# A fused three-block transformer kernel whose TensorE no longer multiplies constants between a layer norm and the projection behind it

## The chip, the cores and the metric

The kernel runs on one core of a Trainium2 chip. The metric is the time of one execution on the device in microseconds (us). A core has TensorE (PE: matmuls and, as PEld, the loads of the stationary operand), VectorE (DVE), ScalarE (ACT), GpSimd (POOL) and SyncE (SP), which here issues the loads of the weights.

## The reference, cut to what matters

Three different blocks are applied to the same 256 tokens of width 2048, each with its own weights (about 600 MB in fp32 altogether). Each block is a large input projection, three or two token mixers, an output projection, and a residual layer norm; blocks two and three have a feed-forward part with a second layer norm. The change sits where a layer norm is followed by a projection of its result:

```
# block 1, end                          out = merged @ w_o
x = _layer_norm(ALPHA * x + out, ln_g, ln_b)
# block 2                               u = x @ w_in_2, mixers, then:
x = layer_norm(alpha * x + mix @ w_out_2, ln1_g, ln1_b)
gu = x @ w_gate_up_2;  hid = silu(gu[..., :D_FF]) * gu[..., D_FF:]
x = layer_norm(alpha * x + hid @ w_down_2, ln2_g, ln2_b)
# block 3                               proj = x @ w_in_3, mixers, then:
x = layer_norm_3(ALPHA * x + mixed @ w_out_3, ln1_g, ln1_b)
h = square(relu(x @ w_up_3))
x = layer_norm_3(ALPHA * x + h @ w_down_3, ln2_g, ln2_b)
```

The norm subtracts the mean over the 2048 columns of a token, multiplies by the inverse root of the variance, and applies gain and bias. So there are four places where a projection waits for a norm: in front of `cvg0` (first projection of block 2), `gu` (gate and up of block 2), `qkm` (first projection of block 3) and `up3`. The last norm is followed by the output only.

## The kernel before, in words

Every weight passes through a ring of four slots. SyncE loads a chunk of 256 rows by 512 columns, ScalarE rounds it to `w_hi` (L1282), VectorE computes the remainder `w_lo` (L1809), and TensorE multiplies in three products: hi by hi, hi by lo, lo by hi (`products`, L594 to L596; the "wide" kind has L618 for the first two at once and L624 for the third). A tile of a projection has eight chunks of two k-steps each; a chunk is 24 matmuls of 256 columns in the kinds F, or 8 of 512 and 8 of 256 columns in the wide kind.

The activations lie token-major in `xtok`. For a projection they are needed column-major: TensorE transposes them in eight groups (`transpose_x`, L746, four transposes a group, eight matmul rows for two groups), ScalarE copies a group to `x_hi` (L1331, `x_both` in the profile) and VectorE makes `x_lo` from it (L1809, also `x_both`), which frees the group for TensorE (semaphore `xTp_used`).

At a norm the last chunk of the projection ahead is computed in token halves, so that VectorE adds and measures one half (`half_done`) while TensorE computes the other. VectorE then takes the statistics, centres and scales the columns of chunk 0 in two finer quarters (`scaled(0, 2)`), each of which raises `x_cols`, and TensorE transposes group 0 and group 1, one for each. Chunk 0 of the projection then needs group 0 only. Columns for later groups are scaled by VectorE (L1815) while chunk 0 runs, and transposed ahead of chunks 1, 3 and 5.

`project_opening` (L679) writes this order for TensorE. All engines run their streams in program order. With `normed=True` it first waits on `tile_free` of the PSUM tile that the projection will write, then calls `keep_clock` (L674), which multiplies `upper` (a triangle of ones, constant) by the identity into that PSUM tile with start=True; chunk 0 starts the same tile anew, so the product is never read. Eight such products come ahead of the transposes of groups 0 and 1, two behind them. Each fp32 product is two matmul rows of 256 columns in the trace.

The diff touches `keep_clock` and `project_opening` alone. Of the five calls, `aqk` at the program's start is not normed and has no such products; `cvg0`, `gu` (wide), `qkm` and `up3` (wide) have.

Of the kernel before, what the change touches and what calls it, by code (L numbers as in the profile page):

```python
# [16 lines left out]
S = 256  # L17
# [152 lines left out]
def tiles_of(eng, sec, unroll=False, opens=False, closes=False):  # L170

    n, a, b = sec.n, sec.u0, 1 - sec.u0
    pairs = n // 2 - closes
    alone = pairs if unroll else min(1, pairs) if opens else 0
    if pairs - alone == 1:
        alone = pairs
    for i in range(alone):
        yield 2 * i, a, i
        yield 2 * i + 1, b, i
    if alone < pairs:  # L180
        with eng.Fori(alone, pairs) as i:
            yield 2 * i, a, i
            yield 2 * i + 1, b, i
    if closes:
        yield 2 * pairs, a, pairs
        yield 2 * pairs + 1, b, pairs
    if n % 2:
        yield n - 1, a, pairs


def build(nc, I, out):
    plan, widths, landed = plan_weights()
    ctx = ExitStack()
    with ctx:
        free = [-(-nc.sbuf_base // 32) * 32]

        def sb(name, shape, dt=F32, at=None):

            if at is None:
                at = free[0]  # L200
                free[0] += -(-4 * int(np.prod(shape[1:])) // 32) * 32
            return nc.alloc_sbuf_tensor_at(name, shape, dt, offset=at)
# [34 lines left out]
        ident = ident_r[:].bitcast(F32)  # L237
        ones = sb("ones", [P, P])
        upper = sb("upper", [P, S])
# [11 lines left out]
        ps = ctx.enter_context(nc.psum_tensor("ps", [P, 8, 512], F32))  # L251
# [337 lines left out]
        def _(pe):  # L589
# [72 lines left out]
            def stationary(hi, lo, at=0):  # L662

                return lambda c, s: [v[:, at + c * CH:at + (c + 1) * CH, :] for v in (hi, lo)]
# [6 lines left out]
                    tile(kind, u, sec.chunk(u, 0), sec.more(it), sec.chunks, src, width, side=side, halves=halves,  # L671
                         normed_next=norm and t == sec.n - 1)

            def keep_clock(u, times):  # L674

                for i in range(times):
                    pe.matmul(ps[:, 2 * u, 0:S], ident, upper[:, 0:S], start=True, stop=True)

            def project_opening(name, normed=True, side=None, kind="F"):  # L679

                sec, base = plan[name], n.now(xTp_used)
                if normed:
                    pe.wait_ge(tile_free[sec.u0], sec.tiles[sec.u0])
                    keep_clock(sec.u0, 8)
                    transpose_x(range(2), normed)
                    keep_clock(sec.u0, 2)
                else:
                    transpose_x(range(4), normed)
                for t, u, it in tiles_of(pe, sec, side is not None, opens=True):
                    first = isinstance(t, int) and t == 0  # L690
                    pe.wait_ge(tile_free[u], sec.tiles[u] + it)
                    tile(kind, u, sec.chunk(u, 0), sec.more(it), sec.chunks, stationary(x_hi, x_lo), TW,
                         (normed, base) if first else None, None if first else side, at=4 * (u ^ sec.u0))
# [42 lines left out]
            def transpose_x(groups, normed):  # L736

                for g in groups:
                    if normed and (g % 2 == 0 or g == 1):
                        pe.wait_ge(x_cols, n.next(x_cols))  # L740
                    elif g % 2 == 0 and not normed:
                        pe.wait_ge(x_landed[g // 2], 16)
                    pe.wait_ge(xTp_used, max(0, n.now(xTp_used, 1) - 3))
                    for k in range(2):
                        for t in range(2):
                            last = pe.transpose(ps[:, 4 + g % 4, k * S + t * P:k * S + (t + 1) * P].bitcast(F32R),  # L746
                                                xtok_r[:, t, (2 * g + k) * P:(2 * g + k + 1) * P], ident_r[:])
                    last.then_inc(xTp_ready, 1)
# [424 lines left out]

            pe.wait_ge(ident_ready, 1)
            project_opening("aqk", False)
            pe.wait_ge(par_landed, 16 * len(params))
            pe.wait_ge(xTp_used, n.now(xTp_used))
# [5 lines left out]
            for k in range(KT):  # L1183
                for i, (w, x) in enumerate(((alr_hi, x_hi), (alr_hi, x_lo), (alr_lo, x_hi))):
                    last = pe.matmul(ps[0:G_RANK, 6, 0:S], w[:, k, :], x[:, k, :], start=(k == 0 and i == 0),
                                     stop=(k == KT - 1 and i == 2))
# [11 lines left out]
            sec = plan["merge"]  # L1198
# [26 lines left out]
            project("wo", "T", merged, norm=True)  # L1225

            project_opening("cvg0")
            side = second_mixers()
            project("cvg1", "F", side=side, halves=True)
            project("qkv", "F", side=side, halves=True)  # L1230
            project("z", "F", side=side, halves=True)
            project("wout2", "T", in_parts((1, 1, 2, 2, 3, 3, 4, 4)), side=side, halves=True, norm=True)
            project_opening("gu", kind="wide")
            pe.wait_ge(h_primed, AHEAD)
            project("down2", "T", hidden, norm=True)
# [1587 lines left out]
```

## Time and profile before

| | |
|---|---|
| median of 3 runs | 3470.61 us (3467.54 to 3471.84) |
| profiled execution, time | 3468.43 us |
| its span | 3466.6 us (1.8 us outside it) |
| PE busy, share of the span | 3411.7 us, 98% |
| DVE, ACT | 2224.0 us (64%), 1632.0 us (47%) |
| mean granted TensorE clock | 0.996 |
| DMA | 609.04 MB, mean 176 GB/s |

TensorE is busy nearly all the time, so what lengthens its stream lengthens the kernel, and a busier VectorE or ScalarE does so only where TensorE waits for them. The page's waits and timelines show where. A granted clock of 1.00 is the higher of TensorE's two levels (2.4 GHz), 0.50 the lower (1.2 GHz).

### The profile page before, as it was taken

What the parts mean: (1) busy time and instruction counts of PE and PEld (TensorE: products, weight loads), DVE (VectorE), ACT (ScalarE), POOL (GpSimd) and SP (SyncE); (2) the same over time, 40 slices, a digit from 0 to 9 for tenths busy, and PEclk for the clock granted to TensorE, in tenths of its full rate; (3) what the DMA queues carried; (4) which work ended last, traced back from release to release, by engine and by line L of the source; (5) the groups of instructions that cost most, each with busy time, mean ns of one, the idle gap of its engine ahead of it and who ended that gap; (6) DMA issues with size and microseconds to landing.
All of it is one profiled execution on the core that took longest, in us unless ns stands there. A gap on an engine that the chain in (4) does not pass through costs nothing.

```text
span 3466.6 us, 50657 instructions
## 1 busy us (share of the span) xinstructions
PE 3411.7 (98%) x20440; PEld 3037.7 (88%) x20440; DVE 2224.0 (64%) x2895; ACT 1632.0 (47%) x1924; POOL 6.3 (0%) x9
## 2 busy tenths in 40 slices
PE   8999999999999999999999999999999999999998
PEld 8998998888889999888888888899999888888886
DVE  5777655555568997565455566777766645457766
ACT  4445544444434443544444455543444444555554
POOL 0000000000000000000000000000000000000000
PEclk9999999999999999999999999999999999999999
DMA  6454566566655522555655566545446566666664
GB/s 193 146 168 151 157 192 202 193 197 205 215 165 164 158 86 74 187 160 187 193 188 187 187 210 193 182 148 164 152 145 210 156 194 192 188 201 199 194 192 149
DMA packets 324193, 609.04 MB, mean 176 GB/s; under 512 B 28254, under 2 KB 42592, under 8 KB 322729
## 3 DMA queue, kind: packets, MB, share of 16 engines
q1 hardware_dynamic: 317640, 587.45, 54.0%
q10 hardware_dynamic: 6368, 19.01, 1.5%
q8 instruction: 131, 2.15, 0.2%
q14 instruction: 54, 0.43, 0.0%
HBM read 604.29 MB, written 2.10 MB: 175 GB/s over the span
## 4 chain that ended last, share of the span: by engine, by line
PE 90%; DVE 7%; ACT 1%; issue 1%; DMA 1%; SPq 0%; ACTq 0%; DVEq 0%
PE ps L594 20%; PE ps L595 20%; PE ps L596 20%; PE ps L618 16%; PE ps L624 8%; DVE xtok L1815 2%; DVE arena L1815 2%; DVE w_lo L1809 1%; DVE arena L1809 1%; PE ps L1099 1%; DMA ring<-in_w_in 1%; PE ps L1118 0%; ACT w_hi L1282 0%; PE ps L800 0%; PE ps L1115 0%
## 5 line engine op out<-in xcount | busy, mean ns | idle before, releaser
L1809 DVE TENSOR_TENSOR w_lo<-ring,w_hi 128x1024 fp32r<-128x1024 f32 (+2 forms) x1136 | 1367.2, 1209 | 1017.0 <-ACT w_hi L1282 836.5
L1282 ACT ACTIVATE w_hi<-ring 128x1024 fp32r<-128x1024 f32 (+2 forms) x1136 | 1183.3, 1047 | 1551.6 <-PE ps L594 1155.5
L594 PE MATMUL ps<-x_both,w_hi 128*128 128x256 f32 x2368 | 684.4, 289 | 1.7 <-DVE x_both L1809 1.4
L595 PE MATMUL ps<-x_both,w_hi 128*128 128x256 f32 x2368 | 672.3, 284 | 0.0
L596 PE MATMUL ps<-x_both,w_lo 128*128 128x256 f32 x2368 | 672.2, 284 | 0.0
L618 PE MATMUL ps<-x_both,w_hi 128*128 128x512 f32 x2432 | 610.0, 393 | 1.9 <-DVE x_both L1809 1.9
L618 PEld LDWEIGHTS ps<-x_both,w_hi 128*128 128x128 f32 x2432 | 437.4, 189 | 80.9 <-DVE x_both L1809 2.3
L594 PEld LDWEIGHTS ps<-x_both,w_hi 128*128 128x128 f32 x2368 | 456.2, 193 | 7.4 <-issue 4.8
L595 PEld LDWEIGHTS ps<-x_both,w_hi 128*128 128x128 f32 x2368 | 456.5, 193 | 0.8 <-issue 0.5
L596 PEld LDWEIGHTS ps<-x_both,w_lo 128*128 128x128 f32 x2368 | 456.0, 193 | 0.0
L624 PEld LDWEIGHTS ps<-x_both,w_lo 128*128 128x128 f32 x2432 | 331.8, 190 | 23.7
L624 PE MATMUL ps<-x_both,w_lo 128*128 128x256 f32 x2432 | 339.1, 282 | 0.0
L594 PE MATMUL ps<-w_hi,h_hi 128*128 128x512 f32 x864 | 336.5, 389 | 2.0 <-DVE h_lo L1809 2.0
L595 PE MATMUL ps<-w_lo,h_hi 128*128 128x512 f32 x864 | 336.3, 389 | 0.0
L596 PE MATMUL ps<-w_hi,h_lo 128*128 128x512 f32 x864 | 336.3, 389 | 0.0
L594 PE MATMUL ps<-w_hi,x_both 128*128 128x512 f32 (+1 forms) x672 | 259.2, 386 | 0.0
L596 PE MATMUL ps<-w_hi,x_both 128*128 128x512 f32 (+1 forms) x672 | 255.6, 380 | 0.0
L595 PE MATMUL ps<-w_lo,x_both 128*128 128x512 f32 (+1 forms) x672 | 255.4, 380 | 0.0
L594 PEld LDWEIGHTS ps<-w_hi,h_hi 128*128 128x128 f32 x864 | 162.2, 188 | 36.5 <-DVE h_lo L1809 2.8
L595 PEld LDWEIGHTS ps<-w_lo,h_hi 128*128 128x128 f32 x864 | 162.2, 188 | 33.5
L596 PEld LDWEIGHTS ps<-w_hi,h_lo 128*128 128x128 f32 x864 | 162.2, 188 | 33.5
L594 PE MATMUL ps<-w_hi,y_hi 128*128 128x512 f32 x448 | 174.7, 390 | 3.4 <-DVE y_lo L1809 3.4
(356 smaller groups left out, 3253.9 us busy)
## 6 DMA issues: line engine op xcount, KB each, us to landing
ring<-in_w_in SPq DMA_DIRECT2D x416, 512.0 KB, 3.5
ring<-in_w_down SPq DMA_DIRECT2D x216, 512.0 KB, 4.2
ring<-in_w_gate_up SPq DMA_DIRECT2D x176, 512.0 KB, 4.2
ring<-in_w_up SPq DMA_DIRECT2D x128, 512.0 KB, 3.9
ring<-in_w_out SPq DMA_DIRECT2D x64, 512.0 KB, 4.4
ring<-in_w_branch SPq DMA_DIRECT2D x36, 512.0 KB, 4.1
ring<-in_w_in SPq DMA_DIRECT2D x48, 384.0 KB, 3.0
ring<-in_w_o SPq DMA_DIRECT2D x32, 512.0 KB, 4.5
```

The lines of the kernel that those rows point to most:

```text
L594: first = pe.matmul(out, left[0], right[0], start=start, stop=False)
L595: pe.matmul(out, left[0], right[1], start=False, stop=False)
L596: return first, pe.matmul(out, left[1], right[0], start=False, stop=stop)
L618: first = pe.matmul(ps[:, at + e, :], w_hi[:, s, k, e * P:(e + 1) * P], x_both[:, c * CH + k].rearrange("p h s -> p (h s)"), start=(c == 0 ...
L624: last = pe.matmul(ps[:, at + e, 0:S], w_lo[:, s, k, e * P:(e + 1) * P], x_hi[:, c * CH + k, :], start=False, stop=(c == chunks - 1 and k ...
L1099: last = pe.matmul(ps[:, 4 + e, m * P:(m + 1) * P], d_lm[:, 4 * e + m], d_t[:, 8 * f + 4 * e + m], start=True, stop=True)
L1282: last = act.activation(w_hi[:, s, :, 0:width], ring[:, s, :, 0:width], ACT.Copy)
L1809: return dve.tensor_tensor(o, a, b, op)
L1815: return dve.scalar_tensor_tensor(o, a, s, b, op0, op1, **kw)
```

## The change

The helper `keep_clock` and its two calls are deleted. The waits, the transposes, the token halves at the norm, the finer quarter and the two groups ahead of chunk 0 stay as they are, and no other engine's code is touched.

```
             def project_opening(name, normed=True, side=None, kind="F"):
                 sec, base = plan[name], n.now(xTp_used)
                 if normed:
                     pe.wait_ge(tile_free[sec.u0], sec.tiles[sec.u0])
-                    keep_clock(sec.u0, 8)
                     transpose_x(range(2), normed)
-                    keep_clock(sec.u0, 2)
                 else:
                     transpose_x(range(4), normed)
...
-            def keep_clock(u, times):
-                for i in range(times):
-                    pe.matmul(ps[:, 2 * u, 0:S], ident, upper[:, 0:S], start=True, stop=True)
```

TensorE's order before, where the output projection of block 1 (`m_hi`, `m_lo` are its inputs) ends and `cvg0` begins:

```order
L595 MATMUL ps<-w_lo,m_hi 128x512
L596 MATMUL ps<-w_hi,m_lo 128x512
L677 MATMUL ps<-upper,ident_r 128x256 x8
L746 MATMUL ps<-ident_r,xtok_r 128x128 x8
L677 MATMUL ps<-upper,ident_r 128x256 x2
L594 MATMUL ps<-x_both,w_hi 128x256
```

And in the changed kernel, whose lines have moved up by seven:

```order
L595 MATMUL ps<-w_lo,m_hi 128x512
L596 MATMUL ps<-w_hi,m_lo 128x512
L739 MATMUL ps<-ident_r,xtok_r 128x128 x8
L594 MATMUL ps<-x_both,w_hi 128x256
```

Both rows of constants are gone; the transposes now follow the last product directly. It is the same at `qkm`. At `gu` and `up3` the row behind is the wide one; before:

```order
L677 MATMUL ps<-upper,ident_r 128x256 x8
L746 MATMUL ps<-ident_r,xtok_r 128x128 x8
L677 MATMUL ps<-upper,ident_r 128x256 x2
L618 MATMUL ps<-x_both,w_hi 128x512 x8
L624 MATMUL ps<-x_both,w_lo 128x256 x8
```

The rest of TensorE's stream is the same, 14112 rows before and 14104 now, and nothing moves on the other engines.

## Rows read from the trace of the kernel before

**Rows 1.** The page: busy time, granted clock by slice, chain that ended last.
```profile
PE 3411.7 (98%) x20440; PEld 3037.7 (88%) x20440; DVE 2224.0 (64%) x2895; ACT 1632.0 (47%) x1924; POOL 6.3 (0%) x9
...
PE 90%; DVE 7%; ACT 1%; issue 1%; DMA 1%; SPq 0%; ACTq 0%; DVEq 0%
```
**Rows 2.** Instructions of line 677: count, duration in ns (minimum/median/maximum), starts.
```profile
L677 PE MATMUL ps<-upper,ident_r x80: 377/379/634, 986.9 to 2738.4; 128*128 128x256 f32 x80
```
**Rows 3.** Timeline of PE at cvg0: start, length, operation, [idle before <-releaser], in us.
```profile
986.91 3.61 PE L677 MATMUL ps<-upper,ident_r 128*128 128x256 f32 x16
992.62 0.53 PE L746 MATMUL ps<-ident_r,xtok_r 128*128 128x128 f32 x4 [2.09 <-DVE xtok L1815]
993.41 0.53 PE L746 MATMUL ps<-ident_r,xtok_r 128*128 128x128 f32 x4 [0.26 <-DVE xtok L1815]
993.77 1.10 PE L677 MATMUL ps<-upper,ident_r 128*128 128x256 f32 x4
994.61 0.39 PE L594 MATMUL ps<-x_both,w_hi 128*128 128x256 f32 x1
...
998.12 0.88 PE L746 MATMUL ps<-ident_r,xtok_r 128*128 128x128 f32 x8 [0.39 <-DVE xtok L1815]
```
**Rows 4.** Chain of waits in time order at cvg0, and VectorE's timeline row of the same place.
```profile
994.60 0.69 DVE x_both L1809
...
993.81 1.48 DVE L1809 TENSOR_TENSOR x_both<-ps,x_both 128x512 fp32r<-128x512 f32 x2 [0.46 <-ACT x_both L1331]
```
**Rows 5.** Timeline of PE at qkm.
```profile
2239.42 3.61 PE L677 MATMUL ps<-upper,ident_r 128*128 128x256 f32 x16
2246.25 0.53 PE L746 MATMUL ps<-ident_r,xtok_r 128*128 128x128 f32 x4 [3.22 <-DVE xtok L1815]
...
2248.35 0.78 PE L594 MATMUL ps<-x_both,w_hi 128*128 128x256 f32 x1
...
2252.75 0.80 PE L746 MATMUL ps<-ident_r,xtok_r 128*128 128x128 f32 x8
```
**Rows 6.** Windows: busy time (xcount) of PE, PEld, DVE, ACT, POOL; granted clock; DMA share; GB/s.
```profile
990.35:994.61 4.26, 1.91 (x14) 1.44 (x13) 3.66 (x9) 1.43 (x3) 0.00 (x0) 1.00 0.00 0
...
2247.96:2251.37 3.41, 3.41 (x16) 3.24 (x15) 3.28 (x6) 1.30 (x2) 0.00 (x0) 0.50 0.00 0
...
1264.93:1268.33 3.40, 3.17 (x15) 3.18 (x16) 2.19 (x4) 0.60 (x1) 0.00 (x0) 0.50 0.08 12
...
1495.08:1502.79 7.71, 5.36 (x29) 4.29 (x28) 6.97 (x17) 1.49 (x3) 0.00 (x0) 1.00 0.25 88
2730.78:2738.48 7.70, 5.34 (x29) 4.28 (x28) 6.97 (x16) 1.49 (x3) 0.00 (x0) 1.00 0.30 98
```
**Rows 7.** Timeline of PE around 1265 us, in block 2.
```profile
1265.16 3.56 PE L1099 MATMUL ps<-arena 128*128 128x128 f32 x16 [3.04 <-DVE arena L1809]
```
**Rows 8.** Timeline of PE at the program's start.
```profile
6.33 1.23 PE L746 MATMUL ps<-ident_r,xtok_r 128*128 128x128 f32 x8 [6.33 <-DMA xtok<-in_x]
...
10.98 0.54 PE L594 MATMUL ps<-x_both,w_hi 128*128 128x256 f32 x1
...
15.37 0.41 PE L596 MATMUL ps<-x_both,w_lo 128*128 128x256 f32 x1
15.58 0.32 PE L594 MATMUL ps<-x_both,w_hi 128*128 128x256 f32 x1
...
18.26 0.28 PE L595 MATMUL ps<-x_both,w_hi 128*128 128x256 f32 x1
18.38 0.28 PE L596 MATMUL ps<-x_both,w_lo 128*128 128x256 f32 x1
```
**Rows 9.** Timeline of PE at gu.
```profile
1502.79 2.11 PE L618 MATMUL ps<-x_both,w_hi 128*128 128x512 f32 x8
...
1506.31 0.88 PE L746 MATMUL ps<-ident_r,xtok_r 128*128 128x128 f32 x8 [0.46 <-DVE xtok L1815]
...
1517.27 2.12 PE L618 MATMUL ps<-x_both,w_hi 128*128 128x512 f32 x8 [0.94 <-DVE x_both L1809]
```

More of the change, by code:

```diff
@@ L672, in project @@
                          normed_next=norm and t == sec.n - 1)
-            def keep_clock(u, times):
-                for i in range(times):
-                    pe.matmul(ps[:, 2 * u, 0:S], ident, upper[:, 0:S], start=True, stop=True)
             def project_opening(name, normed=True, side=None, kind="F"):
@@ L683, in project_opening @@
                     pe.wait_ge(tile_free[sec.u0], sec.tiles[sec.u0])
-                    keep_clock(sec.u0, 8)
                     transpose_x(range(2), normed)
-                    keep_clock(sec.u0, 2)
                 else:
```

## Prediction

> **What bounds the kernel now.** I read the page first. PE is busy for 98% of the span and makes up 90% of the chain that ended last [rows 1]: TensorE sets the time, so the question is what its stream loses or gains at the places that the diff touches. Next I read the instructions of line 677 [rows 2]: 80 matmul rows, that is 10 products of two rows at each of four openings (cvg0, gu, qkm, up3). Then the timeline of PE at one of them, cvg0 [rows 3]. The reader should see that it is not TensorE that is late there. The first 16 rows of constants start the moment the last product is issued and take 3.6 us; after them PE still sits idle for 2.09 us, then for 0.26 us, until VectorE delivers normalised columns. Only from chunk 0 on (994.61) does PE work in earnest, and 3.51 us later, at the transposes ahead of chunk 1, it waits once more for VectorE, 0.39 us. So the constants stand in time that is otherwise idle, and what they can do is act on TensorE's clock. That is why the windows view comes last, for its granted clock [rows 6].
>
> **The change, part by part.**
>
> *The eight products ahead of the transposes.* They are removed: 4 x 16 rows at 0.22 us each (3.61 us for 16), 3.5 us of PE time per opening. The cover is the norm on VectorE, which ends 2.09 us after them at cvg0 and 3.22 us after them at qkm [rows 3, 5]. Direct gain: nothing, at any of the four.
>
> *The two products behind the transposes.* They are removed too: four rows, 0.84 us from 993.77 to the start of chunk 0 at 994.61 [rows 3]. What they hide is the way of group 0 through ScalarE and VectorE. VectorE starts the first of its two x_both instructions at 993.81 and the second at 994.60 [rows 4], so the first result, which chunk 0 needs, is there between 994.5 and 994.6, and chunk 0 starts at 994.61. The products cost at most 0.1 us there. I take 0.05 us for each opening, 0.2 us in all; the bounds are 0 and 0.5 us. Nothing else waits behind them: no semaphore is raised by them.
>
> *What their absence does to the clock.* This is the term that matters, and no row shows an opening without constants. Before, cvg0, gu and up3 went through the gap up to chunk 0 at a granted clock of 1.00 [rows 6]. Without the constants PE has nothing from 986.9 to 994.5 at cvg0 but eight rows of transposes: 7.6 us. Two rows of this trace say what such a gap leads to. In block 2 PE waited 3.04 us for VectorE [rows 7], and the stretch of 3.4 us behind it ran at 0.50 [rows 6]. At qkm, whose norm comes 1.1 us later than the others, the idle time was 3.22 us in spite of the constants, and the clock was 0.50 from 2247.96 to 2251.37 [rows 5, 6]. Gaps with more than twice that idle time should fall to the lower level every time. I take it that all four do.
>
> *What a low opening costs.* The lower bound is qkm itself. From the start of chunk 0 to the next transposes it took 2252.75 - 2248.35 = 4.40 us [rows 5], cvg0 at full clock 998.12 - 994.61 = 3.51 us [rows 3]. The difference is 0.9 us: the matmuls were slower, but the 0.39 us wait for VectorE was swallowed. The upper bound comes from the program's start, where PE came out of idleness as it will now: the low clock lasted until 15.58, 4.6 us after the first product at 10.98, with matmuls 0.21 us apart instead of 0.12 [rows 8]. A chunk 0 wholly at that pace takes 24 x 0.21 = 5.1 us. The transposes ahead of it are slower as well: eight rows took 1.23 us there against 0.88 us [rows 8, 3], 0.35 for eight, so some 0.2 us for the four of a group, through which ScalarE and VectorE are reached later. Chunk 0 would begin at 994.8 and end at 999.9 in place of 998.12: 1.8 us, and 2.1 us if the transposes behind it are low as well. Where in the gap the clock falls decides between 0.9 and 2.1; the only full opening without constants (the start) speaks for the upper half and the only one at a norm for the lower, so I take 1.3 us. Wide openings are priced alike: chunk 0 is 3.52 us from start to transposes with a wait of 0.46 us in it [rows 9]. The later wait of 0.94 us at 1517.27 does not take the loss back, since VectorE, which ends it, is fed by the transposes that come late.
>
> *The sum.* cvg0, gu and up3 turn from full to low: 3 x 1.3 = 3.9 us (bounds 2.7 and 6.3). qkm was low already and has a longer gap now: 0.4 us more (bounds 0 and 1.2). The constants give back 0.2 us. Together +4.1 us on the profiled execution of 3468.43 us: 3472.5 us. The profiled execution lies 2.2 us below the median of 3470.61 us, but part of that distance may be openings of before that fell low in other executions, which would shrink the step there. I go half the way: 3473.5 us, +2.9 us or +0.08% on the median. The noise of the three runs is 4.3 us from end to end. A measurement of this kernel tells a change from none at about 0.2%, 6.9 us, so my forecast is within it.
>
> **The rivals.**
>
> *The clock does not fall, or does so as often as before.* For it: the level before was full through 2.09 us of idle time, and only one such gap in four fell. Against it: 3.04 and 3.22 us of idle time fell both times, and now there are over 5 us without a row of any kind. It would leave the 0.2 us gain: 3470.4 us, and 3468.2 us if the profiled execution is taken as the base. It is also the case in which the change does nothing at all to the path.
>
> *The clock comes back late* (the slower side). The place is chunk 1 and, in the F openings, chunk 2, where PE no longer waits for anyone, so that every low microsecond costs in full. If the clock stays low for one more stretch of 3.4 us at each opening, 3.4 x (1 - 0.12 / 0.21) = 1.5 us is lost on top of 2.1: 3.6 us an opening, 14.4 us in all, less the 0.9 that qkm pays already: +13.3 us, 3483.9 us. It decides (over 6.9 us in all) from a mean cost of 2.0 us an opening, which is when the clock comes back some 5 us or more after chunk 0 starts. For it: at the program's start it took 4.6 us, close to that point, and it had been low through the transposes too [rows 8]. Against it: at qkm and at 1265 us the low stretch was over after 3.4 us [rows 6], and the start had further pauses for the input ahead of its first chunk.
>
> On the same side stands a rule of the Trainium skill, page "TensorE: Matmul & The Clock Gate", section "Terms": the penalty is the throttled time multiplied by the share of clock pulses held back, which is a half at the lower level. By that rule 3.41 us at 0.50 would cost 1.7 us and two such stretches at each opening 3.4 us, 3.4 x 4 - 1.7 = +11.9 us in all, 3482.5 us. The row of qkm speaks against counting so: its 3.41 low microseconds cost 0.9 us, because 0.39 us of them came ahead of chunk 0 and TensorE had another 0.39 us of waiting to give away.
>
> *The constants cost more than they seem to.* If ScalarE and VectorE were ready well ahead of 994.6 and the second set was what chunk 0 waited for, removing it would give up to 0.84 us an opening, 3.4 us in all: 3467.2 us with the clock unhurt. Against it: the x_both rows end at that very moment [rows 4]. Even then it is not faster by 0.2%.
>
> **How the numbers follow.** All four openings low at 0.9 to 2.1 us: 0.62, forecast 3473.5 us, own range 3470 to 3478. Clock unhurt: 0.17, about 3470. Clock late: 0.16, from 3478 up; I cut its far end. Constants on the path: 0.02. Something not in the profile, either side: 0.03. The range of 3467.5 to 3480 us takes in the first, second and fourth case with the spread of the runs shown, and the near part of the third. Slower by over 0.2% (above 3477.5): the third case and a tail of the first, together 0.16, since part of the third stays below its price. Faster by over 0.2% (below 3463.7): 0.03. Within: 0.81.
>
> **What would show it.** In the changed profile: a granted clock of 0.50 in the stretch around the start of cvg0, gu, qkm and up3; idle time of 5.7 us (6.8 at qkm) ahead of the first transposes; first matmuls of chunk 0 spaced 0.21 us; from the start of chunk 0 to the next transposes 4.4 to 5.3 us in place of 3.5, without the 0.39 us wait; and chunk 0 starting 0.1 to 0.2 us later relative to the norm's last product, or 0.05 us earlier if the fall comes after it. The forecast is wrong if an opening keeps 1.00, if low stretches reach into chunk 2, or if the waits of VectorE for PE move so that the loss is made good behind the opening, by the next norm at the latest.

## The result and the profile after

| | before | after |
|---|---|---|
| median | 3470.52 us (3467.48 to 3473.63, 22 runs) | 3475.70 us (3472.55 to 3478.53, 22 runs) |
| ratio | | 1.0014, 95% interval 1.0008 to 1.0020 |
| profiled execution, span | 3468.43 us, 3466.6 us | 3475.74 us, 3473.9 us |
| mean granted clock | 0.996 | 0.991 |

The changed kernel is slower by 5.2 us at the median, 0.15%; the interval excludes zero and goes from 2.8 to 6.9 us. The forecast was 3473.5 us in a range of 3467.5 to 3480 us.

First the page of the kernel after: busy time of each engine. TensorE has less to do, and yet the kernel takes longer:

```profile
PE 3403.8 (98%) x20360; PEld 3030.2 (87%) x20360; DVE 2223.9 (64%) x2895; ACT 1632.3 (47%) x1924; POOL 6.3 (0%) x9
```

PE lost 80 rows against [rows 1], and 7.9 us of busy time. (The page counts 20440 rows before and 20360 now; the counts of 14112 and 14104 given with the change stand in no view of the trace.) VectorE and ScalarE have the same work. Now the four openings in the timeline of PE (start, length, operation, idle before it), each with its first transposes and those ahead of chunk 1:

```profile
992.82 1.50 PE L739 MATMUL ps<-ident_r,xtok_r 128*128 128x128 f32 x8 [5.59 <-issue]
995.01 0.55 PE L594 MATMUL ps<-x_both,w_hi 128*128 128x256 f32 x1 [0.69 <-issue]
...
1503.09 1.50 PE L739 MATMUL ps<-ident_r,xtok_r 128*128 128x128 f32 x8 [5.59 <-issue]
1505.27 3.75 PE L618 MATMUL ps<-x_both,w_hi 128*128 128x512 f32 x8 [0.68 <-issue]
...
1510.05 0.80 PE L739 MATMUL ps<-ident_r,xtok_r 128*128 128x128 f32 x8
...
2249.99 1.49 PE L739 MATMUL ps<-ident_r,xtok_r 128*128 128x128 f32 x8 [6.71 <-issue]
...
2257.23 0.81 PE L739 MATMUL ps<-ident_r,xtok_r 128*128 128x128 f32 x8
...
2742.59 1.50 PE L739 MATMUL ps<-ident_r,xtok_r 128*128 128x128 f32 x8 [5.59 <-issue]
```

The idle time of 2.09 us of [rows 3] is now 5.59 us (6.71 us at qkm), and the wait of 0.39 us ahead of the transposes of chunk 1 is gone: it is TensorE that is late. The eight wide matmuls at gu take 3.75 us in place of 2.11 [rows 9]. The windows view gives the clock (length; busy time of PE, PEld, DVE, ACT, POOL; granted clock; DMA share; GB/s):

```profile
987.20:990.60 3.40, 0.03 (x1) 0.00 (x0) 3.26 (x8) 0.15 (x1) 0.00 (x0) 1.00 0.59 178
990.64:1000.86 10.22, 7.33 (x38) 7.01 (x38) 8.09 (x14) 2.36 (x4) 0.00 (x0) 0.50 0.03 3
1502.64:1509.44 6.80, 5.64 (x19) 4.56 (x20) 5.98 (x10) 2.25 (x3) 0.00 (x0) 0.50 0.00 1
2246.74:2256.96 10.22, 6.25 (x30) 5.94 (x31) 9.09 (x18) 2.55 (x4) 0.00 (x0) 0.50 0.07 24
2741.68:2748.48 6.80, 5.18 (x17) 4.10 (x18) 5.98 (x11) 2.25 (x3) 0.00 (x0) 0.50 0.00 0
2482.26:2489.06 6.80, 6.80 (x21) 5.64 (x21) 1.35 (x2) 2.61 (x3) 0.00 (x0) 0.50 0.29 84
```

All four openings stand in a low stretch, of 6.8 or 10.2 us, where before had one of 3.4 us at qkm [rows 6]. The last row is no opening: it lies in block 3 and begins while 24 matmul rows of one column, which sum squares per head, are running. There before kept its full clock. The same matmuls of the two timelines, side by side in time, before first, after below:

```profile
2475.68 2.84 PE L901 MATMUL ps<-ones,arena 128*128 128x1 f32 x24
2478.38 0.48 PE L594 MATMUL ps<-w_hi,x_both 128*128 128x512 f32 x1
2478.69 0.39 PE L595 MATMUL ps<-w_lo,x_both 128*128 128x512 f32 x1
```
```profile
2480.16 3.41 PE L894 MATMUL ps<-ones,arena 128*128 128x1 f32 x24
2483.43 0.77 PE L594 MATMUL ps<-w_hi,x_both 128*128 128x512 f32 x1
2484.00 0.63 PE L595 MATMUL ps<-w_lo,x_both 128*128 128x512 f32 x1
```

I set the 20360 matmul rows that both kernels have against each other and took the difference of their starts. It is +0.2 us up to cvg0 and grows by 2.1 us there, 1.4 us at gu, 0.8 us at qkm (which was low before too) and 1.2 us at up3: 5.6 us at the openings. It grows by 3.2 us more at the one-column rows at 2480 us, and shrinks by 1.6 us at 2572 us, where before had a low stretch and after has none. Together 7.3 us (the parts are rounded), the difference of the spans. A delay made at an opening is not made good behind it: the difference stays as it is up to the next of these places.

### The profile page after: what moved, and what is told of

The parts are those of the page before. It is cut to its first block, busy times and chain, and to the rows that moved or that the text cites. A ratio compares the mean times of both kernels' runs of the same rounds, so it can differ in the third digit from the quotient of the medians.

```text
span 3473.9 us, 50497 instructions
## 1 busy us (share of the span) xinstructions
PE 3403.8 (98%) x20360; PEld 3030.2 (87%) x20360; DVE 2223.9 (64%) x2895; ACT 1632.3 (47%) x1924; POOL 6.3 (0%) x9
## 4 chain that ended last, share of the span: by engine, by line
PE 91%; DVE 6%; issue 1%; ACT 1%; DMA 1%; SPq 0%; ACTq 0%; DVEq 0%
PE ps L594 20%; PE ps L596 20%; PE ps L595 20%; PE ps L618 16%; PE ps L624 8%; DVE arena L1808 2%; DVE w_lo L1802 1%; DVE xtok L1808 1%; DVE arena L1802 1%; PE ps L1092 1%; DMA ring<-in_w_in 1%; PE ps L1111 0%; PE ps L793 0%; PE ps L1108 0%; PE ps L764 0%
```

## Experiments

One measure runs through all of them: the time from the start of the last product of the norm's projection to the start of the transposes ahead of chunk 5, read from PE's timeline at each opening. Where the clock stays up throughout (run e8 below) it is 25.4 us at cvg0, 25.3 at gu, 26.5 at qkm and 25.3 at up3. The table gives what each kernel's profiled execution loses against that.

| kernel | products ahead, behind | cvg0 | gu | qkm | up3 | sum, us | median of times, us |
|---|---|---|---|---|---|---|---|
| before | 8, 2 | 0.0 | 0.0 | 0.9 | 0.0 | 0.9 | 3470.5 |
| before, second profile (e11) | 8, 2 | 0.6 | 0.0 | 0.9 | 0.0 | 1.5 | |
| after | 0, 0 | 2.1 | 1.4 | 1.7 | 1.2 | 6.5 | 3475.7 |
| after, second profile (e12) | 0, 0 | 1.7 | 2.0 | 2.1 | 1.5 | 7.3 | |
| e1 front gone | 0, 2 | 1.6 | 2.0 | 0.5 | 0.5 | 4.6 | 3475.5 |
| e2 behind gone | 8, 0 | 0.8 | 0.8 | 1.8 | 0.0 | 3.5 | 3473.3 |
| e3 one column | 16, 4 of one column | 1.6 | 1.8 | 1.9 | 2.1 | 7.5 | 3476.1 |
| e4 gap filled | 12 (15), 2 | 0.0 | 0.0 | 0.0 | 0.0 | 0.0 | 3469.2 |
| e5 half dose | 4, 1 | 0.5 | 1.4 | 0.2 | 1.1 | 3.2 | 3470.5 |
| e6 after, wide sums | 0, 0 | 2.0 | 1.4 | 1.7 | 1.1 | 6.2 | 3472.7 |
| e7 filled, wide sums | 12 (15), 2 | 0.0 | 0.0 | 0.0 | 0.0 | 0.0 | 3467.2 |
| e8 three places | 12 (15), 2 | 0.0 | 0.0 | 0.0 | 0.0 | 0.0 | 3465.8 |
| e9 quiet, with | 8, 2 | 0.0 | 0.0 | 0.9 | 0.9 | 1.8 | 3468.2 |
| e10 quiet, without | 0, 0 | 2.1 | 1.4 | 1.7 | 1.1 | 6.3 | 3470.7 |

The number in brackets is that of qkm. The runs were timed in three groups, each on one chip together with the kernel before: e1 to e4 (before 3470.5 us), e5 to e8 (before 3470.4 us), e9 and e10 (before 3468.3 us). A comparison across the groups is weaker than one within a group.

The edits of the first four are to the kernel before, lines of `project_opening` and `keep_clock` only.

### e1: only the products ahead removed

```
                     pe.wait_ge(tile_free[sec.u0], sec.tiles[sec.u0])
-                    keep_clock(sec.u0, 8)
                     transpose_x(range(2), normed)
                     keep_clock(sec.u0, 2)
```

> The eight products ahead of the transposes are removed at each of the four openings, the two behind them stay. Clock theory: TensorE idles 5.7 us (6.8 us at qkm) ahead of the transposes, the granted clock is 0.50 at chunk 0 in all four openings, and from the last product to the transposes ahead of chunk 1 it takes 12.7 to 13.5 us at cvg0, gu and up3 (11.4 us before), 14 to 14.8 us at qkm. Time +4 to +6 us on before, as in the changed kernel; the two products behind may add 0.3 us an opening, since they now run at the low clock too. Rival, the products behind matter as much as those ahead (they carry TensorE from the transposes into chunk 0): the openings lose half as much, +2 to +3 us. Rival, chance: the openings lose nothing, 11.4 us each, and the time is within 1 us of before.

Measured: 3475.47 us (3472.61 to 3475.98, 10 runs), ratio 1.0009 (1.0000 to 1.0019). All four openings low. The timeline of PE at cvg0:

```profile
993.06 1.50 PE L745 MATMUL ps<-ident_r,xtok_r 128*128 128x128 f32 x8 [5.59 <-issue]
994.35 2.04 PE L677 MATMUL ps<-upper,ident_r 128*128 128x256 f32 x4
...
1000.20 0.80 PE L745 MATMUL ps<-ident_r,xtok_r 128*128 128x128 f32 x8
```

The two products behind now take 2.04 us in place of 1.10 [rows 3], and push chunk 0 out: it starts 8.75 us after the last product, 8.17 us in the changed kernel. At qkm and up3 the low stretch ended early, and these openings lost 0.5 us only, below what was expected: 4.6 us at the openings against 6.5 us in the changed kernel, in one profile of each. By the times the two products behind save nothing visible once the eight are gone: the median is that of the whole change.

### e2: only the products behind removed

```
                     transpose_x(range(2), normed)
-                    keep_clock(sec.u0, 2)
```

> Only the two products behind the transposes are removed, the eight ahead stay. Clock theory: 3.5 us of products break the gap, so most openings stay at 1.00; an opening at which the clock falls costs 1 to 2 us. Chunk 0 starts 0.05 us earlier or at the same time. Time 0 to +2 us on before. If the products behind were a cost of their own on the path: -0.4 us or better, up to -3.4 us. If they matter as much as those ahead: +2 to +3 us.

Measured: 3473.25 us (3467.43 to 3476.54, 10 runs), ratio 1.0007 (0.9997 to 1.0016): unclear at the median, +2.8 us. The profile shows more than was expected of them: three of four openings fell. The windows view has cvg0 at full clock up to chunk 0, low through it, gu low through chunk 0 as well, and qkm for twice as long:

```profile
986.60:994.40 7.80, 4.78 (x26) 3.73 (x25) 7.06 (x17) 1.49 (x3) 0.00 (x0) 1.00 0.31 89
994.44:997.82 3.38, 3.38 (x16) 3.38 (x17) 3.35 (x6) 1.06 (x1) 0.00 (x0) 0.50 0.00 0
1503.04:1506.42 3.38, 3.38 (x14) 3.00 (x13) 3.35 (x5) 0.56 (x1) 0.00 (x0) 0.50 0.00 0
2247.15:2253.95 6.80, 6.30 (x32) 6.15 (x33) 5.25 (x7) 1.94 (x3) 0.00 (x0) 0.50 0.00 0
```

Chunk 0 starts 7.93 us after the last product at cvg0, as before to 0.01 us: the products behind were wholly hidden. They are not without effect on the clock, though: with them 1 or 2 of the four openings fell (before, e11, e9), without them three, if in one profile only.

### e3: the same instructions with one column

```
-                    pe.matmul(ps[:, 2 * u, 0:S], ident, upper[:, 0:S], start=True, stop=True)
+                    pe.matmul(ps[:, 2 * u, 0:1], ident, upper[:, 0:1], start=True, stop=True)
...
-                    keep_clock(sec.u0, 8)
+                    keep_clock(sec.u0, 16)
...
-                    keep_clock(sec.u0, 2)
+                    keep_clock(sec.u0, 4)
```

> The same gaps are filled by products of one column in place of 256, twice as many (16 ahead, 4 behind) so that TensorE's queue is occupied about as long as before: 32 rows at 0.11 us, 3.6 us. Clock theory: TensorE has instructions but its array does next to nothing, so the clock falls as in the changed kernel: 0.50 at chunk 0 of all four openings, 12.7 to 13.5 us from last product to the transposes ahead of chunk 1, time +4 to +6 us. Rival, what the constants keep is TensorE's instruction stream (fetch, queue, first loads after a pause) and not its array: openings as before, 11.4 us, time within 1 us of before.

Measured: 3476.10 us (3473.50 to 3480.74, 10 runs), ratio 1.0016 (1.0007 to 1.0026). The timeline of PE at cvg0, then the windows of cvg0 and gu:

```profile
987.28 3.63 PE L677 MATMUL ps<-upper,ident_r 128*128 128x1 f32 x32
992.99 1.54 PE L746 MATMUL ps<-ident_r,xtok_r 128*128 128x128 f32 x8 [2.08 <-DVE xtok L1815]
```
```profile
992.06:998.84 6.78, 5.81 (x29) 5.62 (x30) 5.97 (x11) 2.25 (x3) 0.00 (x0) 0.50 0.01 2
1500.64:1507.42 6.78, 6.25 (x24) 5.39 (x25) 5.97 (x11) 2.25 (x3) 0.00 (x0) 0.50 0.00 1
```

TensorE is occupied as long as before (3.63 us against 3.61) and idle as long as before (2.08 against 2.09), and yet all four openings are low. This tells the two theories apart: a stream of instructions and a pause of the same length do not keep the clock up, where products of 256 columns did at three of the four openings. The kernel is as slow as the changed one, but not by the clock alone: the eight short rows behind the transposes take 1.83 us at the low clock and push chunk 0 out to 8.97 us after the last product, 0.8 us later than in the changed kernel.

### e4: the gap filled

```
-                    keep_clock(sec.u0, 8)
+                    keep_clock(sec.u0, 15 if name == "qkm" else 12)
```

> Twelve products ahead of the transposes in place of eight, fifteen at qkm, so that TensorE is idle some 0.5 us there. Clock theory: no opening falls to 0.50, qkm takes 12.6 us from last product to the transposes ahead of chunk 1 in place of 13.6, all others 11.4; time -0.5 to -1.5 us on before at the median. Rival, eight are enough and the low clock at qkm comes from elsewhere: qkm unchanged, time the same as before. If the added products reach past the norm they delay the transposes, up to +0.3 us an opening.

Measured: 3469.20 us (3466.24 to 3471.55, 10 runs), ratio 0.9996 (0.9987 to 1.0006): not told from before by the times. By the profile no opening fell. The timeline of PE at qkm, and a window over the opening:

```profile
2240.08 6.63 PE L677 MATMUL ps<-upper,ident_r 128*128 128x256 f32 x30
2246.91 0.54 PE L746 MATMUL ps<-ident_r,xtok_r 128*128 128x128 f32 x4 [0.19 <-DVE xtok L1815]
...
2252.43 0.87 PE L746 MATMUL ps<-ident_r,xtok_r 128*128 128x128 f32 x8 [0.39 <-DVE xtok L1815]
```
```profile
2240.00:2253.00 13.00, 12.16 (x75) 10.51 (x73) 12.22 (x23) 2.56 (x4) 0.00 (x0) 1.00 0.26 79
1410.41:1417.19 6.78, 6.01 (x14) 4.78 (x15) 5.26 (x5) 3.02 (x5) 0.00 (x0) 0.50 0.48 153
```

qkm has its 0.39 us wait back and takes 12.57 us from last product to the transposes ahead of chunk 1 (13.57 before): the 0.9 us that I had taken as the price of one low opening is confirmed by its removal. The second window is a low stretch in another place, behind a wait of 3.44 us for y_lo in the output projection of block 2. The kernel before waits there just as long, at full clock in its profile; its row:

```profile
1413.36 0.47 PE L594 MATMUL ps<-w_hi,y_hi 128*128 128x512 f32 x1 [3.44 <-DVE y_lo L1809]
```

By the starts of the common rows the low stretch costs e4 2.8 us there, and a second one, of 3.4 us at 2478.8 us behind the one-column rows, 1.6 us. So the clock falls at these two places also in a kernel whose openings all keep it.

### e5: half as many products

```
-                    keep_clock(sec.u0, 8)
+                    keep_clock(sec.u0, 4)
...
-                    keep_clock(sec.u0, 2)
+                    keep_clock(sec.u0, 1)
```

> Four products ahead of the transposes and one behind, in place of eight and two: 1.7 us of products, then some 3.8 us idle. Clock theory: the openings fall to 0.50 as in the changed kernel, or nearly as often; the low stretch ends earlier or later with its place. From last product to the transposes ahead of chunk 1: 12 to 13.5 us at cvg0, gu, up3. Time +3 to +5 us on before. Rival, a proportional effect of the products: +2 to +3 us. Rival, any product is enough: within 1 us of before.

Measured: 3470.50 us (3469.26 to 3471.94, 10 runs), ratio 1.0001 (0.9991 to 1.0010). The expectation of +3 us missed. The profile does show all four openings low, with 3.2 us lost in them, 1.7 to 2.3 more than in before's two profiles, but its time of 3471.94 us is the highest of the ten. The granted clocks of all ten runs are 0.993 or 0.994, while before's 33 go from 0.994 to 0.996. So half the products leave TensorE at the low clock for longer in every run, and the times still can't tell the kernel from before. Why the added low time costs so little at the median is open.

### e6 and e7: the sums of block 3 widened

In the kernel after (e6) and in the one with filled gaps (e7):

```
-   last = pe.matmul(ps[:, at - 1 + k, 2 * h + t:2 * h + t + 1], src[:, h, t * P:(t + 1) * P], ones[:, 0:1],
+   last = pe.matmul(ps[:, at - 1 + k, 2 * h + t:2 * h + t + 96], src[:, h, t * P:(t + 1) * P], ones[:, 0:96],
```

> The changed kernel with one other edit, in block 3: the 24 and 16 matmul rows of one column (line 894 there) stream 96 columns of ones in place of one; every row overwrites all but the first column of the row before it, so the sums are as they were, and a row still takes 0.11 us. Theory: the part of the step that lay outside the openings, the 6.8 us low stretch behind these rows at 2482 us (+3.0 us) that before did not have in its profile, and before's own low stretch at 2572 us, are chances of where the clock falls and not effects of the change. With these rows wide no low stretch starts at 2478 to 2484 or 2570 to 2580 us; time 1 to 3 us below the changed kernel, 3473 to 3475 us, with the openings as in the changed kernel (+5 us). Rival, the change itself causes the low stretch at 2482: it stays.

> Twelve products ahead of the transposes (fifteen at qkm), two behind, and the wide rows of sums in block 3. Clock theory: no opening falls, no low stretch at 2476 to 2580 us; what is left is at 1140, 1265 and at times 1412 us. Time 3466 to 3468.5 us, 2 to 4 us below before at the median, and the two clusters of before's times (3468 and 3473 us) come closer together. Rival, the low stretches elsewhere are made up for later: same as with the filled gaps alone, 3469 us.

Measured: e6 3472.70 us (3469.76 to 3475.12, 10 runs), ratio 1.0008 (0.9999 to 1.0018); e7 3467.22 us (3463.99 to 3471.50, 11 runs), ratio 0.9990 (0.9981 to 0.9999). The windows and the timeline of e6:

```profile
2476.00:2486.00 10.00, 9.90 (x59) 8.43 (x58) 5.88 (x12) 5.26 (x6) 0.00 (x0) 1.00 0.36 106
2568.00:2578.00 10.00, 9.97 (x64) 9.65 (x63) 4.44 (x5) 5.14 (x6) 0.00 (x0) 1.00 0.52 154
990.37:1000.57 10.20, 7.00 (x35) 6.69 (x35) 8.40 (x15) 2.55 (x4) 0.00 (x0) 0.50 0.00 0
```
```profile
2479.86 2.92 PE L894 MATMUL ps<-ones,arena 128*128 128x96 f32 x24
```

24 rows of 96 columns take 2.92 us, of one column 2.84 us: the width is nearly free. The 24 weight loads of these rows take 2.75 us in before and in e6, so the rows seem to go at their pace. Both low places of block 3 are at full clock, the openings fall as before this edit, and the median is 3.0 us below the changed kernel's, which was timed in another group. Row by row against the changed kernel's profile, e6 is 3.2 us earlier from the sums on. So some 3 us of the changed kernel's profiled time was lost behind the sums, outside the openings.

In e7 all four openings kept the clock, and apart from the program's end, which is low in every kernel, the only low stretches are at 1138.5 and 1264.8 us, 3.4 us each. Its time is in the range expected.

### e8: a third place filled

On e7, ahead of the wait for y_lo in the first tile of the output projection of block 2:

```
+                first = [True]
...
+                    if c == 2 and first[0]:
+                        first[0] = False
+                        u = 1 - plan["wout2"].u0
+                        pe.wait_ge(tile_free[u], plan["wout2"].tiles[u])
+                        keep_clock(u, 7)
                     pe.wait_ge(y_part, parts[c])
```

> As the run before it, and seven products more in the output projection of block 2, where TensorE waits 3.44 us for y_lo (1409.5 to 1413.4 us). Clock theory: no low stretch at 1410 to 1418 us, which the run with filled gaps had for 6.8 us at a cost of 2.8 us. Time 0 to 1.5 us below the run without them at the median, 3465.5 to 3468 us. If the products reach past the wait they cost up to 0.3 us.

Measured: 3465.77 us (3463.94 to 3465.89, 11 runs), ratio 0.9987 (0.9978 to 0.9996): 4.6 us below before, timed with it, and 9.9 us below the changed kernel of another group, by the medians. The runs lie within 2 us of each other, before's 33 beside them within 6.3. The windows of cvg0, qkm and the y_lo wait:

```profile
986.00:998.00 12.00, 10.99 (x68) 9.44 (x67) 11.22 (x22) 2.56 (x4) 0.00 (x0) 1.00 0.22 67
...
2239.00:2252.00 13.00, 12.16 (x76) 10.53 (x74) 12.23 (x23) 2.71 (x5) 0.00 (x0) 1.00 0.25 77
...
1408.00:1414.00 6.00, 5.66 (x26) 4.54 (x25) 4.70 (x5) 5.97 (x9) 0.00 (x0) 1.00 0.40 124
```

This is the fastest kernel of the study. The low stretches that it keeps are at 1138 and 1264 us, each 3.4 us, and the one at the program's end.

### e9 and e10: the change alone, with the other places quiet

e9 is e8 with `keep_clock(sec.u0, 8)` ahead, as before; e10 has neither call at the openings. They differ by the two calls that the change of this study deletes and by nothing else.

> The openings as in the kernel before (eight products ahead, two behind); outside them the wide rows of sums and the seven products at the y_lo wait, which take away three of the places at which the clock can fall by chance. With the next kernel it gives the cost of the change alone. Clock theory: the openings cost what they cost before (0 to 1.5 us in all over the filled ones), time 3466 to 3467.5 us at the median, with less spread than before.

> The same with no products at the four openings, as in the changed kernel. Clock theory: all four openings low, from last product to the transposes ahead of chunk 1 12.6 to 13.5 us (14.3 at qkm); 4.5 to 6 us above the kernel with them, 3470.5 to 3473 us, with an interval that excludes zero clearly since the low stretches elsewhere no longer add their chance. Rival, part of the measured 5.2 us came from elsewhere (the low stretch at 2482 us): 2 to 3.5 us above the kernel with them.

Measured: e9 3468.15 us (3467.31 to 3470.49, 11 runs), e10 3470.74 us (3470.06 to 3472.74, 11 runs), in one group on one chip. Their difference is 2.6 us; resampling the 11 and 11 times gives an interval of 1.8 to 4.0 us. Against before they are 0.9995 (0.9986 to 1.0004) and 1.0002 (0.9993 to 1.0012). e9 was expected at 3466 to 3467.5 us and missed that by 0.7 us. The windows of e10 at its openings, and of e9 at the two of its four that fell:

```profile
990.38:1000.58 10.20, 7.13 (x36) 6.82 (x36) 8.26 (x14) 2.53 (x4) 0.00 (x0) 0.50 0.01 1
1502.38:1509.16 6.78, 5.60 (x19) 4.52 (x20) 5.97 (x10) 2.25 (x3) 0.00 (x0) 0.50 0.00 1
```
```profile
2247.70:2251.08 3.38, 3.38 (x16) 3.22 (x15) 3.24 (x6) 1.14 (x2) 0.00 (x0) 0.50 0.00 0
2735.81:2739.19 3.38, 3.38 (x9) 2.65 (x9) 3.24 (x6) 1.66 (x2) 0.00 (x0) 0.50 0.00 0
```

The profiled executions differ by 4.5 us in their openings and by 4.9 us in their time (3467.31 and 3472.19 us). At the median it is less: e9's profiled execution is its fastest, e10's is one of its three slowest (3472.2 to 3472.7 us, granted clock 0.992), and of the other eight (3470.1 to 3470.9 us) seven have a granted clock of 0.993. The difference lies in the range of the rival of the expectation (2 to 3.5 us) and not in that of the theory (4.5 to 6 us): about half of the 5.2 us stays when the other places are quiet. Whether the rest was made at those places, or the openings themselves cost less in most executions than in the profiled one, these two runs do not tell.

### e11 and e12: both kernels once more

> The kernel before, unchanged, one more look. Its times lie in two clusters, near 3468 and near 3473 us, and its first profile is of the lower one. Theory: the clusters differ by where the clock falls by chance. If this look is of the upper cluster, its low stretches cover a place that the first did not (the sums at 2478 or the y_lo wait at 1412 us, 2.8 to 3 us each, or an opening, 0.9 to 1.5 us), and their cost adds up to the difference; if it is of the lower one, the list of low stretches is like the first's. Rival: the time differs without a difference in low stretches.

> The changed kernel, unchanged, one more look. All four openings fall again, with 1.2 to 2.1 us lost at each by the transposes ahead of chunk 7 tiles on, 5 to 7 us in all over a kernel with filled gaps. Near 3473 us if no low stretch stands behind the sums at 2482 us, near 3476 us if it does. Rival: an opening stays at 1.00 in some executions, then it takes 11.4 us to the transposes ahead of chunk 1.

Measured, one profiled execution each: before 3469.01 us, after 3478.26 us. Before is again of the lower cluster, so its upper one was not seen in a profile. cvg0 fell this time, in spite of its constants; after has all four low, and lost 3.5 us more outside them than before's first profile. Windows of before's second profile at cvg0, then of after's at the y_lo wait and at gu:

```profile
992.61:995.99 3.38, 3.30 (x14) 2.76 (x15) 2.60 (x6) 1.19 (x2) 0.00 (x0) 0.50 0.00 0
```
```profile
1413.27:1420.05 6.78, 5.94 (x14) 4.71 (x15) 5.33 (x5) 3.06 (x4) 0.00 (x0) 0.50 0.46 152
1502.02:1512.22 10.20, 7.12 (x28) 6.03 (x28) 8.28 (x14) 2.55 (x4) 0.00 (x0) 0.50 0.02 6
```

## Why the prediction was right, point by point

**TensorE's products ahead stood in idle time**: right. The time from the last product to the first transposes is 5.9 to 6.0 us with and without them (7.1 us at qkm).

**The products behind cost at most 0.1 us**: right, and 0.05 us was still too much; e2 shows 0.01 us.

**All four openings fall**: right in every profile of a kernel without constants (after, e6, e10, e12: 16 of 16 openings). The prediction argued it from the idle time alone. e3 shows that idle time is not the whole of it: with the idle time of before and rows of one column all four fall too.

**0.9 to 2.1 us an opening, taken at 1.3**: the bounds held, with measured losses of 2.1, 1.4, 1.7 and 1.2 us. The mean of 1.6 us says that 1.3 us was too low; the middle of the bounds, 1.5 us, would have been nearer. The parts are as worked out: chunk 0 starts 0.25 us later (0.2 expected), matmuls are 0.21 us apart, from the start of chunk 0 to the next transposes it takes 5.3, 4.8, 5.1 and 4.6 us (4.4 to 5.3 expected), and the wait of 0.39 us (0.46 us at gu) is the only thing that is swallowed. In VectorE's and ScalarE's work nothing made the loss good.

**The sum**, +4.1 us on the profiled execution, came out as 5.6 us at the openings, 3 x 1.3 having been 4.7 in fact and the 0.4 at qkm 0.8. Against the median I took 2.9 us, with the argument that some of before's openings fall in other executions. That they do is shown (cvg0 in e11, up3 in e9), but the median moved by 5.2 us. The step of 2.6 us with the other places quiet is near 2.9 us partly by luck, since the profiles of that pair differ by 4.9 us. Nor does it say much that the time came out within the range: 3467.5 to 3480 us holds the time of before as well. What bears the prediction out is the granted clock and the loss at each opening.

**What the sum left out** are the low stretches outside the openings. The prediction treated the clock elsewhere as given. In after's two profiles it fell at the sums at 2482 us (3.2 us in the first) or at 1413 us and behind the sums, in before's two profiles only behind the second group of sums at 2572 us (1138 and 1265 us, where it fell in most profiles of any kernel, apart). Taking these places away lowered the changed kernel's median by 5.0 us across the groups (3475.7 to 3470.7), and that of the kernel with constants by 0.2 us in one group (3468.3 to 3468.2) or 2.4 us against the 22 runs of the result. By the medians something like half of the measured 5.2 us goes with them; by the first pair of profiles it is 1.6 us of 7.3 (3.2 us more at 2482 us, 1.6 us less at 2572 us). How large this part is stays open. So does whether the change makes these falls likelier: e4, with all its openings at full clock, had them at 1410 and 2479 us, so the low openings are not needed for them. It may be that the changed kernel's delays move these places in time, or that the runs drew them unevenly. No run here tells the two apart.

**The late clock** (the rival on the slower side) did not take place as priced, but it was closer than its chance of 0.16 said: at cvg0 and qkm the clock came back 5.9 and 4.8 us after chunk 0 had started, at cvg0 behind the end of chunk 0, and e12 had three openings with a low stretch of 10.2 us. None reached chunk 2. (Its price of 13.3 us is the 14.4 us less 0.9 less the 0.2 us of the constants, which the text of the prediction does not name.) The four low stretches are 34.0 us long together and cost 6.5 us: 15.5 us of them lay ahead of the start of chunk 0, which they put off by 0.25 us an opening only, and at each opening a wait of 0.39 or 0.46 us was swallowed. By the penalty rule of the Trainium skill ("TensorE: Matmul & The Clock Gate", section "Terms") the estimate for 34.0 low microseconds would be 17 us; the measurement does not agree.

**The clock unhurt**, at 0.17: refuted for a kernel without any constants. The pause of 2.09 us in before's cvg0 was harmless in the first profile with products of 256 columns on both sides of it; in e11 the same opening fell, and e3, with the same pause and rows of one column, fell at all four.

## What to carry to other kernels

When TensorE bounds a kernel, a pause in which it waits for another engine can cost twice: once while it lasts and again behind it, while the clock is low (1.2 to 2.1 us an opening here). Matmuls on constants in such a pause are worth it if they are wide (256 columns here) and end before the real data arrive, and they should fill the pause nearly whole: 8 products ahead and 2 behind, with a pause of 5.6 us (6.7 us at qkm), left it to chance (1 or 2 of 4 openings low), 12 (15 at qkm) and 2 did not (no opening low in three kernels, one profile of each). Read the granted clock of every stretch behind a pause or behind rows of few columns, and compare two kernels in several executions, since falls at other places add their own microseconds to the difference that is meant.

## What the runs showed of the hardware that was not expected

- Matmul rows of one column did not keep the clock up: with 3.63 us of them in each gap it fell as without any instruction (e3). In the changed kernel a low stretch of 6.8 us that cost 3.2 us began within 24 of them at 2480 us. Of the nine profiles with these rows of one column six have a low stretch there (before, e11 and e3 have none); of the five with rows of 96 columns, which took 2.92 us in place of 2.84, none has (e6 to e10).
- The spread of the times of one kernel goes with the granted clock of its executions. Of the 86 runs of before beside the experiments, the 39 with a granted clock of 0.996 take 3467.2 to 3469.2 us, the 12 with 0.995 take 3470.0 to 3472.7 us, and the 35 with 0.994 take 3472.1 to 3474.0 us. A difference of 0.002 over the span is, by estimate, some 14 us more at half the clock. Where it falls in the slower executions is not shown, since both profiles of before are of the faster ones; the kernel with three places filled, whose runs lie within 2 us, suggests these places.
